# Bidirectional delta-rule scan: heads change partition halves in token space, and the two products of the state are issued in turns

## What is computed

```python
def step(S, inp):
    r_t, w_t, k_t, v_t, kk_t, a_t = inp
    sa = jnp.einsum('bdhvk,bdhk->bdhv', S, -kk_t)
    S = (S * w_t[..., None, :] + sa[..., None] * (kk_t * a_t)[..., None, :]
         + v_t[..., None] * k_t[..., None, :])
    return S, jnp.einsum('bdhvk,bdhk->bdhv', S, r_t)
```

## Time and profile before

| | us |
|---|---|
| median of 3 runs | 4665.88 |
| lowest and highest | 4664.48, 4666.93 |
| span of the profiled execution, first to last instruction | 4657.5 |
| TensorE matmuls busy in it | 4252.3 |
| VectorE, ScalarE busy | 2695.4, 1889.1 |

### The profile page before, as it was taken

How to read it: one execution, slowest core, us unless ns; L and a number is a source line. 1 busy time by engine, 2 the same in 40 slices (tenths; PEclk the granted TensorE clock), 3 DMA queues, 4 the chain that set the end, 5 groups by cost and what they waited for, 6 DMA issues and landing times. The chain is left out here.

```text
span 4657.5 us, 137485 instructions
## 1 busy us (share of the span) xinstructions
PE 4252.3 (91%) x61184; PEld 3660.8 (79%) x61184; DVE 2695.4 (58%) x4665; ACT 1889.1 (41%) x3496; POOL 4.6 (0%) x10
## 2 busy tenths in 40 slices
PE   6999979999998899999999899889999789999988
PEld 2888868888885799766668899877988678888858
DVE  5433657777775653355556433467425577777755
ACT  5333325555554532355554000155333245555542
POOL 0000000000000000000000000000000000000000
PEclk8999989999999999899999999999999899999999
DMA  7444763333325132100000221112446733323341
GB/s 293 150 125 130 229 220 93 93 86 96 92 76 197 64 79 56 52 1 2 1 6 32 95 95 66 53 59 76 120 127 209 241 109 94 99 85 97 85 184 64
DMA packets 543468, 480.78 MB, mean 103 GB/s; under 512 B 30369, under 2 KB 501665, under 8 KB 535201
## 3 DMA queue, kind: packets, MB, share of 16 engines
q1 hardware_dynamic: 411040, 405.91, 27.7%
q10 hardware_dynamic: 131840, 66.07, 4.9%
HBM read 337.94 MB, written 128.71 MB: 100 GB/s over the span
## 5 line engine op out<-in xcount | busy, mean ns | idle before, releaser
L654 PE MATMUL ps<-big_r,stage_r 128*128 128x384 f32 x2976 | 639.7, 349 | 15.7 <-DVE big_r L916 14.2
L654 PEld LDWEIGHTS ps<-big_r,stage_r 128*128 128x128 f32 x2976 | 522.4, 189 | 70.4 <-issue 25.1
L2531 PE MATMUL ps<-big_r,w_out 128*128 128x384 f32 x2304 | 417.6, 341 | 36.6 <-DVE w_out L2647 36.1
L2531 PEld LDWEIGHTS ps<-big_r,w_out 128*128 128x128 f32 x2304 | 406.7, 191 | 45.7 <-DVE w_out L2647 39.3
L654 PE MATMUL ps<-big_r,w_slab_r 128*128 128x384 f32 x1488 | 341.3, 337 | 0.0
L371 PE MATMUL ps<-big_r,stage_r 128*128 128x384 f32 x1536 | 311.0, 337 | 13.8 <-DVE big_r L358 13.8
L2253 DVE TENSOR_REDUCE extra<-ps 128x1 f32<-128x1152 f32 (+1 forms) x144 | 177.7, 1234 | 205.0 <-PE ps L2158 205.0
L371 PEld LDWEIGHTS ps<-big_r,stage_r 128*128 128x128 f32 x1536 | 269.7, 188 | 29.3 <-issue 26.7
L1510 ACT COPY arena<-ps 128x512 f32<-128x512 f32 x288 | 169.1, 587 | 255.5 <-PE ps L1315 255.2
L654 PEld LDWEIGHTS ps<-big_r,w_slab_r 128*128 128x128 f32 x1488 | 267.9, 189 | 0.0
L1664 DVE COPY_PREDICATED arena<-arena,ps 128x128 f32<-128x128 uint32 x720 | 192.8, 324 | 116.7 <-PE ps L1303 115.8
(11 more groups left out here) (260 smaller groups left out, 8079.7 us busy)
## 6 DMA issues: line engine op xcount, KB each, us to landing
w_slab<-in_w SPq DMA_DIRECT2D x138, 512.0 KB, 3.7
arena<-scan_in SPq DMA_DIRECT2D x144, 320.0 KB, 3.8
arena<-scan_in SPq DMA_DIRECT2D x288, 128.0 KB, 3.8
scan_in<-x_resid ACTq DMA_DIRECT2D x48, 576.0 KB, 4.7
arena<-scan_in SPq DMA_DIRECT2D x48, 576.0 KB, 7.2
arena<-scan_in SPq DMA_DIRECT2D x144, 192.0 KB, 4.0
arena<-in_w_ada SPq DMA_DIRECT2D x24, 1024.0 KB, 5.9
x_resid<-in_w_ada SPq DMA_DIRECT2D x24, 1024.0 KB, 5.1
```

What stands on the lines that cost most here:

```text
L654: mm = pe.matmul(g.ps[:, 3 * s + c, 0:CW], w[:, k * P:(k + 1) * P], x[:, k, chunk(c)], start=k == i == 0, stop=k == NB - 1 and i == 2)
L2531: mm = pe.matmul(g.ps[:, bank(i, b), 0:wide[i]], w[:, b, k * P:(k + 1) * P], r, start=k == j == 0, stop=k == NB - 1 and j == 2)
```

## The change

In token space the two heads change places. What `inverse_start` leaves for head h = 0 now lies where that for h = 1 lay, and the other way round (`ps` columns at L1282, output half at L1290). `level_u` reads the Gram matrix of the other head to match, `values` writes the other partition half, and `chain_sa` reads `rhs_sb` and `xt` from the other half. ScalarE and VectorE instructions stay as they are.

By this the matmuls at L1379 have their output in the half opposite to their operands: they use the two quarters off the diagonal, still with bank 5 for both. L1388 stays on the diagonal with bank 7. And the two are issued in turns: two matmuls of the first, two of the second, for each of the four `u`. The signal `rhs_mm` now comes with the 14th of the 16 matmuls; before, it came with the 8th. The number of matmuls, their sizes and all waits are the same.

```diff
@@ inverse_start
-mm = pe.matmul(strided(ps, u * P + h * HD, (1, HD), rows=HALVES[p]),
+mm = pe.matmul(strided(ps, u * P + (1 - h) * HD, (1, HD), rows=HALVES[p]),
                strided(y1, h * 256 + u * HD, (1, HD), rows=HALVES[p]),
...
-mm = pe.matmul(strided(ps, (1 + p) * 512, (1, 256), rows=HALVES[h]), g.ident[HALVES[p], HALVES[p]],
+mm = pe.matmul(strided(ps, (1 + p) * 512, (1, 256), rows=HALVES[1 - h]), g.ident[HALVES[p], HALVES[p]],
@@ level_u
-               strided(gr[q % 3], (1 - p) * 1024 + h * 512 + u * P, (1, HD), rows=HALVES[p]),
+               strided(gr[q % 3], (1 - p) * 1024 + (1 - h) * 512 + u * P, (1, HD), rows=HALVES[p]),
@@ values
-mm = pe.matmul(strided(ps, (3 + t) * 512 + u * HD, (1, HD), rows=HALVES[h]),
+mm = pe.matmul(strided(ps, (3 + t) * 512 + u * HD, (1, HD), rows=HALVES[1 - h]),
@@ chain_rhs
 for s in range(2):
     for d in range(2):
+        u, b = 2 * d + s, 2 * slot(c) + s
         for h in range(2):
-            u, b = 2 * d + s, 2 * slot(c) + s
-            mm = pe.matmul(strided(ps, 5 * 512 + u * HD, (1, HD), rows=HALVES[h]),
+            mm = pe.matmul(strided(ps, 5 * 512 + u * HD, (1, HD), rows=HALVES[1 - h]),
                            strided(ar[c % 4], u * 256 + tau(d, step) * P, (1, HD), rows=HALVES[h]),
                            strided(S, d * 512 + b * HD, (1, HD), rows=HALVES[h]), start=True, stop=True)
-mm.then_inc(rhs_mm, 1)
-
-for s in range(2):
-    for d in range(2):
+        if s == d == 1:
+            mm.then_inc(rhs_mm, 1)
         for h in range(2):
-            u, b = 2 * d + s, 2 * slot(c) + s
             pe.matmul(strided(ps, 7 * 512 + u * HD, (1, HD), rows=HALVES[h]),
                       strided(S, d * 512 + b * HD, (1, HD), rows=HALVES[h]),
...
@@ chain_sa
-               strided(xt[c % 2], lx(d, p, s), (1, HD), rows=HALVES[h]),
-               strided(rhs_sb, u * HD, (1, HD), rows=HALVES[h]), start=True, stop=True)
+               strided(xt[c % 2], lx(d, p, s), (1, HD), rows=HALVES[1 - h]),
+               strided(rhs_sb, u * HD, (1, HD), rows=HALVES[1 - h]), start=True, stop=True)
```

## The result

The changed kernel takes 4675.42 us (median of 8 runs, 4664.04 to 4680.64) against 4664.93 for the kernel before on the same footing (8 runs, 4660.20 to 4666.93). The ratio is 1.0023, with a 95% interval of 1.0013 to 1.0033: slower by 10 us. The forecast was 4665 us in a range of 4657 to 4671. It read rightly when L1303 starts at both places, and missed what the new order set off elsewhere.

What follows compares the result with a forecast made beforehand. The prediction took the ring of L1303, VectorE, L1315 and ScalarE as the bound, with TensorE's products only filling its gaps. Terms -0.7 - 0.3 = -1.0 us against span 4657.5 plus 8.4 gave 4665 us, no change, range 4657 to 4671.

Steps and rivals of the forecast that it cites:

- What bounds the places: At both `chain_rhs` places, copies on ScalarE or VectorE, not TensorE's products, set L1303's start; gain at most 0.7 us.
- Place 1: Between L1315 and L1303 of the fourth level: ScalarE's copy L1510 bounds, distance stays 1.40 us, gain at most 0.7 us.
- place 2: Between L1290 and L1303 of the first level: VectorE's copy L1728 bounds, L1379 to L1303 stays 1.08 us, gain 0.
- The later signal: `rhs_mm` after 28 of 32 records, at 0.45 us instead of 0.46, delays nothing at either place: cost 0.
- the swapped halves: L1290 starting with the other output half could move its end by 4 us either way; taken as 0.
- rival 5: The four quarters don't overlap and a call stays at 0.89 us: 4667 us, 8%.
- rival 1: Slower: row halves sharing banks 5 and 7 exclude each other, a call takes 1.79 us: 4778 us, 3%.
- Stalls of issue: Stalls inside a call are softened by its slack: 0.3 us gained in all, 4 us as lower end.
- Rival 2, the clock: Slower: TensorE's load falls, so its clock drops to 1.2 GHz; one spell in each pair 119 us, 4785 us, 2%.
- the 8.4 us: Time around the profiled span of 4657.5 us, added to reach the median of 4665.88 us.
- Rivals 3 and 4: Faster: TensorE is the bound, 4611 us, 3%; or L1290's order and softened stalls gain a little, 4657 us, 4%.
- the 55 us freed: TensorE time freed by four quarters in turns, 0.38 us in each of 144 `chain_rhs` calls.

Runs made afterwards that it cites:

- e1: Changed kernel with the head swap alone, both calls issued in sequence instead of in turns: 4663.21 us, ratio 1.0006 to the kernel before.
- e15: The changed kernel run and profiled once more, nothing altered: 4675.29 us, ratio 1.0031 to the kernel before.
- e2: Changed kernel with turns only in the first level's call, between L1290 and L1303: 4671.17 us, ratio 1.0028 to the kernel before.
- e13: Changed kernel with each matmul of the first product streaming its columns twice, same instruction count: 4670.39 us, ratio 1.0017 to the kernel before.
- e3: Changed kernel with turns only in the fourth level's call, between L1315 and L1303: 4663.88 us, ratio 1.0011 to the kernel before.
- e4: Kernel before with the scan's raw loads shrunk to 1 KB each from the fifth pair on: 4613.49 us, ratio 0.9905 to the kernel before.
- e5: Changed kernel with the scan's raw loads shrunk to 1 KB each from the fifth pair on: 4619.42 us, ratio 0.9915 to the kernel before.
- e14: Changed kernel with two more matmuls of 224 columns behind the turns, into unused columns: 4667.97 us, ratio 1.0017 to the kernel before.
- e8: Changed kernel with loads issued a pair earlier and turns only between L1290 and L1303 of the first level: 4679.90 us, ratio 1.0043 to the kernel before.

## Why the prediction was wrong

- *What bounds the places*: right for L1303, which starts where it did, with 0.24 and 0.44 us of idle time ahead of it where 0.2 and 0.4 were forecast. Place 1 has 1.40 as forecast. The sign named for place 2, L1379 to L1303 at 1.08 or within 0.06 of it, failed: 1.24 stood, since the swap lets the products start 0.17 us earlier, for which the prediction had no term. A call takes 0.43 us at place 1 and 0.57 at place 2, first start to last, where 0.51 was taken.
- *The later signal, the swapped halves*: right as to cost; L1674 still starts 0.60 us behind the copy's start, the way from L1282 to L1303 moved by 0.01 us, and e1 is within 0.06%. The two quarters more did overlap, so neither rival 5 nor rival 1 came, and the Trainium skill's sentence on row tiles and one PSUM bank (TensorEngine Tiling, Gotcha 1: PSUM Pressure) is not what these runs show for tiles that write different partition halves of the bank: four quarters over banks 5 and 7 started 32 records in 0.43 us.
- *"Stalls of issue ... I take 0.3 us in all"*: the step that failed. It looked at a stall as something that a call's slack could only soften, and so its bound reached down alone. The runs showed 5 to 13 us more of them in the scans (24.7 to 37.4, and 29.9 in e15). At the one place where they came up, inside the second level's L1303, it is 13.3 and 5.0 us where there was nothing, and turns at place 2 make them (8.9 in e2, 10.7 in e13, 1.1 in e3), under the loads (4.4 and 11.5 in all in e4 and e5). The rows for it were there: 24.7 us of "issue" in the lines of the scan, at packet ends, while the loads run, so a term that a new order of TensorE's work can move either way. The range should have reached up by it as it did down.
- *Rival 2, the clock*, had 2%: it may have come in part. The rows against it were a pair without a chain and without a stall; but in the scans the clock fell to 1.2 GHz mostly behind stalls. In the changed kernel's profile 8 of the 12 stalls of over a microsecond had such a spell within 8 us, in that of before 3 of 7. It isn't a rule, since in e2 it is 3 of 13. There are 18 to 29 us more at 1.2 GHz, of which e13 and e14 gave most back with some 3 to 6 us of time; half of the extra time, the bound by the prediction's 1.7 us for each 3.4 us, is 9 to 14.
- *The sums*: the 8.4 us that were put around the span are 1.8 of fixed time and 6.6 by which this execution was quicker than the median; the forecast of no change doesn't hang on it. The upper end of the range, 4665 + 4 + 1.2, is 4670.
- *Rivals 3 and 4* did not come: nothing of the 55 us freed came through by itself.

What stays open is how the turns delay a fetch: it starts later though its packet is used up earlier, it does so with a stretched call and with the loads shrunk too, and e8 is slow with turns away from the loads. How the 10 us are shared between stalls and clock is open as well.

## What to carry to other kernels

Here work taken from an engine that waits at both places gave nothing, and it wasn't free either: the new order changed when the engine's instructions were fetched, and with it the time lost waiting for them. Where "issue" rows add up to more than the effect you look for, put them into the range in both directions. And time that was freed has to be given to work on the path before it counts: here the same turns that cost 0.2 to 0.3% alone are part of a kernel that is 0.5% faster.

## What the runs showed of the hardware that was not expected

TensorE's instructions come in 16 KB packets, one for 126 matmul records here. In the stalls of the first scan TensorE went on only 1.2 to 1.7 us after a packet's transfer had ended. Under a train of loads the start of such a fetch varied from 2.6 to 5.7 us into a pair. Shrinking the loads took 44 us (1%) off the kernel and five sixths of its issue waits in the scans (24.7 to 4.4 us). Two kernels that differ only in the order of sixteen matmuls, e1 and e2, both start L1303 2.47 us into nearly every pair, and lie 0.2% apart in time. Turns at place 2 made the next fetch start about 1 us later or more under the loads, and 1.1 us with the loads shrunk. Matmuls on the two quarters off the diagonal started 0.17 us sooner behind L1290 than those on the diagonal.
